# Seventeen of the up projection's 22 gate/value pairs by seven half products instead of eight

## The chip, the core and the metric

The kernel runs on one core of a Trainium2 chip. The metric is device time in microseconds for one execution of the whole program, median of several runs; lower is better. TensorE (PE) multiplies, VectorE (DVE), ScalarE (ACT) and GpSimd (POOL) work on rows of 128 partitions, SyncE (SP) issues most DMAs. Every engine takes its instructions in program order and waits on semaphores where the program says so.

## The reference

Two layers of a decoder on 520 tokens (512 of a prompt, 8 samples), model width 1024. The part that the change touches is the ConvFFN of each layer:

```
xn    = rms_norm(x, ffn_pre)                       # 520 x 1024
gate, value = xn @ w_up[:, :2816], xn @ w_up[:, 2816:]
h     = gelu(conv3(gate) + bias) * value           # causal convolution over tokens, width 3
x     = x + rms_norm(h @ w_down, ffn_post)
```

The last two gate rows of the prompt and of every sample are outputs too. All matrices are float32.

## The kernel before, in words

Activations lie transposed: 128 features on the partitions, 520 tokens in the free dimension, kept as two halves of 260 (`HALF`). A weight matrix comes as chunks of 128 x 1024 floats (512 KB), one DMA each on SP, into a ring of three (`ring`). Each float32 operand is split in two of a reduced format: ScalarE copies a chunk to its high part (`split_w` in the scalar block, L1479), VectorE subtracts that from the chunk to get the low part (L1882, in place of the chunk), and `w_hi`, `w_lo` count them. A product is then three matmuls: high by high, high by low, low by high (L925, L926, L927 in `dense_tile`), each of 128 x 128 weights by 260 columns. An output tile (128 features, both halves) takes 8 blocks x 2 halves x 3 = 48 matmuls in a pair of PSUM banks; three such pairs take turns, and `evac_a`, `evac_v` tell TensorE when one is free.

The up projection has 22 pairs of tiles, gate i and value i. `dense_front` makes the first three tiles in an order that lets it start before all of the input is there (L946, L947, L955); `dense_tile` the other 41. The input's halves are `hm_hi` (ScalarE, L1492) and `hm_lo` (VectorE, L1896); the norm's factor `rstd` is applied after the product. For pair i VectorE takes the gate out of PSUM (L2420), runs the convolution (`conv`: L2404 to L2408, of which the two with 8 columns are for the samples), multiplies it after ScalarE's gelu (L1801) by `rstd` (L2431), and by the value tile out of PSUM (L2433) into `hf`. Two weight splits a pair lie between. GpSimd does only three small copies a pair, the rows that are outputs (L1832 to L1834), and `ffn_t` tells VectorE that the buffer `gx` may be overwritten two pairs later. `hf` is split in its turn: the first 11 blocks (`EARLY`) during the up projection, the others right after it (L1483 on ScalarE, L1889 on VectorE), since their high parts lie where `hm_hi` and `hm_lo` were. The down projection then has 8 tiles over 22 blocks, three chunks each, and its first tile waits for each block's low part (`s_lo`).

The order on each engine is written out in the loops. The chunks of up and down go through the ring in one sequence, each DMA waiting for the tile three before it (`w_used`).

## Time and profile before

| | us |
|---|---|
| median of 3 runs | 2001.44 |
| lowest, highest | 2000.12, 2002.71 |
| span of the profiled execution, first to last instruction | 1997.6 |
| up projection of the first layer, all but its first three tiles | 624.1 to about 860.7 |
| the same of the second | about 1613 to 1850 |

The profiled execution is told by its span; what lies around the span is in the runs' times and not in the profile: 3.8 us between the span and the median. A row of the profile names an engine, the line of the kernel, the operation, what it writes and reads with shapes, and how often; then its time.

### The profile page before, as it was taken

The page shows a single profiled execution, that of the slowest core. Times are in us where ns is not written, and L with a number is a line of the kernel's source. Part 1 is how long each engine was busy: PE and PEld are TensorE (multiplying, and loading weights), DVE is VectorE, ACT ScalarE, POOL GpSimd, SP SyncE. Part 2 cuts the span into 40 slices and gives each one's busy share as a digit, 9 for nine tenths or more (in the row PEclk, how much of TensorE's full clock was granted, in tenths as well). Part 3 has the DMA queues.
Part 4 walks back from the last instruction along what each step waited for, and adds up shares of the span by engine and source line. Part 5 has one row for each costly group of instructions (what it writes and reads, how often), then busy time and mean ns, then how long its engine had stood idle before and what let it go on. Part 6 is the DMA issues. An engine that isn't in the chain of part 4 may idle for free.

```text
span 1997.6 us, 53462 instructions
## 1 busy us (share of the span) xinstructions
PE 1936.6 (97%) x22496; PEld 1795.0 (90%) x22496; DVE 1241.9 (62%) x2066; ACT 732.4 (37%) x1394; POOL 30.4 (2%) x143
## 2 busy tenths in 40 slices
PE   8999999999999999999999999999999999999997
PEld 7999888776799999999999998887677999999997
DVE  3475868888638665542355767688776476656323
ACT  3223345563634222232232234545636342222321
POOL 0000000000000000000000000000000000000000
PEclk9999999999999999999999999999999999999999
DMA  5225444144222332233342255333442222222332
GB/s 218 88 83 164 149 126 141 55 125 136 87 89 65 95 96 87 94 95 95 101 142 85 75 190 160 113 107 93 128 121 72 78 85 96 86 95 96 96 96 89
DMA packets 153010, 214.29 MB, mean 107 GB/s; under 512 B 18497, under 2 KB 118338, under 8 KB 151362
## 3 DMA queue, kind: packets, MB, share of 16 engines
q1 hardware_dynamic: 134050, 200.38, 31.8%
q10 hardware_dynamic: 18720, 10.49, 1.7%
q8 instruction: 177, 2.90, 0.6%
q14 instruction: 63, 0.52, 0.1%
HBM read 202.58 MB, written 16.59 MB: 110 GB/s over the span
## 4 chain that ended last, share of the span: by engine, by line
PE 77%; DVE 14%; ACT 3%; issue 2%; DMA 2%; ACTq 1%; SPq 0%; DVEq 0%
PE ps L925 18%; PE ps L927 18%; PE ps L926 18%; PE ps L1315 5%; PE ps L1193 1%; DMA ring<-in_w 1%; PE ps L1286 1%; PE ps L1182 1%; PE ps L946 1%; PE ps L947 1%; PE ps L1300 1%; DVE arena L2192 1%; DVE arena L2154 1%; PE ps L1279 1%; PE ps L1195 1%
## 5 line engine op out<-in xcount | busy, mean ns | idle before, releaser
L927 PE MATMUL ps<-hm_hi,ring_lo 128*128 128x260 f32 x1568 | 444.1, 283 | 0.0
L1882 DVE TENSOR_TENSOR ring_lo<-ring,ring_hi 128x1024 fp32r<-128x1024 f32 x130 | 159.3, 1225 | 303.5 <-ACT ring_hi L1479 301.7
L927 PEld LDWEIGHTS ps<-hm_hi,ring_lo 128*128 128x128 f32 x1568 | 296.2, 189 | 0.0
L925 PE MATMUL ps<-hm_hi,ring_hi 128*128 128x260 f32 x1008 | 285.5, 283 | 0.0
L926 PE MATMUL ps<-hm_lo,ring_hi 128*128 128x260 f32 x1008 | 284.6, 282 | 0.0
L1479 ACT ACTIVATE ring_hi<-ring 128x1024 fp32r<-128x1024 f32 x130 | 137.7, 1060 | 319.5 <-DMA ring<-in_w 311.5
L927 PE MATMUL ps<-hf_hi,ring_lo 128*128 128x260 f32 x704 | 198.9, 283 | 0.0
L927 PE MATMUL ps<-in_hi,ring_lo 128*128 128x260 f32 x704 | 198.8, 282 | 0.0
L925 PEld LDWEIGHTS ps<-hm_hi,ring_hi 128*128 128x128 f32 x1008 | 189.6, 188 | 1.8 <-issue 1.8
L926 PEld LDWEIGHTS ps<-hm_lo,ring_hi 128*128 128x128 f32 x1008 | 189.7, 188 | 0.0
L1882 DVE TENSOR_TENSOR ring_lo<-ring,extra_hi 128x1024 fp32r<-128x1024 f32 x64 | 78.4, 1225 | 154.2 <-ACT extra_hi L1479 153.0
L925 PE MATMUL ps<-hm_hi,extra_hi 128*128 128x260 f32 x496 | 140.3, 283 | 0.0
L926 PE MATMUL ps<-hm_lo,extra_hi 128*128 128x260 f32 x496 | 139.9, 282 | 0.0
L927 PEld LDWEIGHTS ps<-hf_hi,ring_lo 128*128 128x128 f32 x704 | 132.6, 188 | 0.0
L927 PEld LDWEIGHTS ps<-in_hi,ring_lo 128*128 128x128 f32 x704 | 132.6, 188 | 0.0
L925 PE MATMUL ps<-in_hi,ring_hi 128*128 128x260 f32 x448 | 128.8, 287 | 1.6 <-DVE ring_lo L1882 1.6
L1479 ACT ACTIVATE extra_hi<-ring 128x1024 fp32r<-128x1024 f32 x64 | 67.8, 1060 | 169.3 <-DMA ring<-in_w 166.6
L925 PE MATMUL ps<-hf_hi,ring_hi 128*128 128x260 f32 x448 | 127.2, 284 | 0.0
L926 PE MATMUL ps<-in_lo,ring_hi 128*128 128x260 f32 x448 | 126.6, 283 | 0.0
L926 PE MATMUL ps<-hf_lo,ring_hi 128*128 128x260 f32 x448 | 126.5, 282 | 0.0
L1716 ACT ACTIVATE arena<-ps,arena 128x128 f32<-128x128 f32 (+3 forms) x128 | 66.2, 526 | 97.6 <-DVEq L442 95.5
L1801 ACT ACTIVATE arena<-arena 128x520 f32<-128x520 f32 x44 | 28.2, 640 | 185.2 <-DVEq L442 185.2
(451 smaller groups left out, 4567.3 us busy)
## 6 DMA issues: line engine op xcount, KB each, us to landing
ring<-in_w SPq DMA_DIRECT2D x200, 512.0 KB, 3.5
extra<-in_kv_cmp SPq DMA_DIRECT2D x96, 128.0 KB, 2.3
arena<-in_kv_cmp SPq DMA_DIRECT2D x80, 128.0 KB, 2.4
slot<-in_kv_cmp SPq DMA_DIRECT2D x80, 128.0 KB, 2.4
out_win_old<-in_win SPq DMA_DIRECT2D x16, 511.0 KB, 4.2
slot<-in_k_sel SPq DMA_DIRECT2D x72, 64.0 KB, 2.0
extra<-in_k_sel SPq DMA_DIRECT2D x72, 64.0 KB, 1.9
arena<-in_v_sel SPq DMA_DIRECT2D x72, 64.0 KB, 2.0
```

What stands on the lines that cost most here:

```text
L925: mmul(out, wh, hi[:, k, cols], start=(k == 0), stop=False)
L926: mmul(out, wh, lo[:, k, cols], start=False, stop=False)
L927: last = mmul(out, wl, hi[:, k, cols], start=False, stop=(ci == len(chunks) - 1 and k == k1 - 1))
L946: mmul(ps[:, banks[i] + h, 0:HALF], w_high(l, n + i)[:, w], hi[:, k, cols], start=(k == 0), stop=False)
L947: last = mmul(ps[:, banks[i] + h, 0:HALF], w_low(l, n + i)[:, w], hi[:, k, cols], start=False, stop=False)
L1182: last = mmul(ps[r, 2, cj * CH:(cj + 1) * CH], gb[r, c, j, 0, :], ww[r, c, j, :], start=True, stop=True)
L1193: last = mmul(ps[r, 0, cj * CH:(cj + 1) * CH], qq[r, c, j, :], zz[r, c, j, :], start=True, stop=True)
L1315: last = mmul(out, w1ss[l][c][:, k, :], slot[:, :, c, k, :], start=(k == 0), stop=(k == STRIDE // 2 - 1))
L1479: A(w_high(l, n), w_place(l, n), ACT.Copy).then_inc(S["w_hi"], 1)
L1716: o.go(A(pp[:, g, cols], ps[:, 4 + g, cols], ACT.Exp, bias=nm[:, q:q + 1], accum_out=sums[:, q:q + 1]))
L1801: o.go(A(cv[:, i % 2, :], cv[:, i % 2, :], ACT.Gelu_apprx_tanh))
L1882: v.tensor_tensor(w_low(l, n), w_place(l, n), w_high(l, n), SUB).then_inc(S["w_lo"], 1)
```

## The change

Each pair of up is 256 output features (gate and value) by 1024 inputs by 520 tokens. It is taken as a 2 x 2 block product: outputs gate and value, inputs the first and second four blocks of 128 (`HK`), tokens the first and second half of 260. Strassen's scheme in Winograd's form gives the four output quarters (gate and value, each half of the tokens) by 7 products of quarter size instead of 8. A quarter product is 4 blocks x 3 = 12 matmuls of 260 columns. Pairs 0 to 4 (`PAIRS = 5`) stay as they were.

- GpSimd makes four sums of weight quarters a pair (`s1` to `s4`, 128 x 512 each), and once a layer the four sums of input quarters (`tf`, 128 x 1040 each), for which it first scales `x` (eight 128 x 520). It also takes over the multiplication by `rstd` (`weigh`).
- ScalarE makes the high part of each of the 7 quarters (`high`), copies PSUM banks into others on which a product then goes on accumulating (`seed` "b", "c"), or into SBUF ("p7", "u4"), and takes the convolution's first tap (`tap`).
- VectorE makes the 7 low parts (`low`), takes the gate out of PSUM by halves (`gate_half`), and adds value quarters from PSUM and SBUF (`val_first`, `val_second`).
- Only 4 blocks of `hf` are split during up (`EARLY = 4`), 18 after it. The chunks of the 17 pairs have slots of their own and their own semaphores. Several semaphores of the first part of the layer are merged (`side_pe`, `side_act`, `side_dve`), with the same waits.

```diff
+PAIRS = 5
+NG = FT - PAIRS
+HK = KB // 2
+LEAD = 4
+def seven_order():
+    out = [(0, "a11")]
+    for g in range(NG):
+        out += [(g, "s2"), (g, "a12"), (g, "s3"), (g, "s1")] + ([(g + 1, "a11")] if g + 1 < NG else []) + [(g, "a22"), (g, "s4")]
+    return out
+SEVEN = seven_order()
...
+        xg = nsa[:].rearrange("p n t -> p (n t)")[:, 0:KB * TOK].rearrange("p (k t) -> p k t", k=KB)
+        tf = hm[:].rearrange("p k t -> p (k t)").rearrange("p (i k t) -> p i k t", i=4, k=HK)
...
+        SEVEN_X = {"a11": ("b11", "a"), "s2": ("t2", "b"), "a12": ("b21", "a"), "s3": ("t3", "e"), "s1": ("t1", "c"), "a22": ("t4", "b"), "s4": ("b22", "c")}
...
+    def gate_load(g):
+        if g >= 2:
+            sp.wait_ge(S["q_pe"], SEVENS * l + SEVEN_AT[g - 2, "a12"])
...
+        sp.dma_start(gate_slot(l, g)[0], I["w"][l, C_UP + 2 * (PAIRS + g)]).then_inc(gate_in[g % 2], 16)
...
+    def product(q):
+        g, name = SEVEN[q]
+        by, letter = SEVEN_X[name]
+        pe.wait_ge(S["q_lo"], QUARTERS * l + TWINS + q + 1)
+        if name == "a11":
+            if g < 2:
+                pe.wait_ge(S["evac_v"], dense_n[0] - 2 + g)
+            else:
+                pe.wait_ge(S["q_gate"], 2 * (NG * l + g - 2) + 1)
+        elif name == "s2":
+            pe.wait_ge(S["q_seed"], SEEDS * l + 4 * g + 1)
+        elif name == "s3" and g >= 2:
+            pe.wait_ge(S["q_val"], 2 * (NG * l + g - 2) + 1)
+        elif name == "s1":
+            pe.wait_ge(S["q_seed"], SEEDS * l + 4 * g + 2)
+        elif name == "s4":
+            pe.wait_ge(S["q_seed"], SEEDS * l + 4 * g + 4)
+        out = ps[:, seven_bank(g, letter), 0:HALF]
+        (hi, lo), wl, wh = moving(by), quarter_full(l, g, name)[1], quarter_high(g, name)
+        for k in range(HK):
+            w = slice(k * P, (k + 1) * P)
+            new = name in ("a11", "s3") and k == 0
+            mmul(out, wh[:, w], hi[:, k, :], start=new, stop=False, skip_group_check=True)
+            mmul(out, wh[:, w], lo[:, k, :], start=False, stop=False, skip_group_check=True)
+            last = mmul(out, wl[:, w], hi[:, k, :], start=False, stop=(k == HK - 1), skip_group_check=True)
+        last.then_inc(S["q_pe"], 1)
+    for q in range(SEVENS):
+        product(q)
+    pe.wait_ge(S["q_gate"], 2 * NG * (l + 1) - 1)
+    pe.wait_ge(S["q_val"], 2 * NG * (l + 1))
...
+    def high(q):
+        if q >= SEVENS:
+            split_w(C_DOWN + q - SEVENS)
+            return
+        g, name = SEVEN[q]
+        if g >= 2:
+            act.wait_ge(S["q_pe"], SEVENS * l + SEVEN_AT[g - 2, name])
+        if name in SUM_AT:
+            act.wait_ge(S["q_sum"], SUMS * l + 1 + 4 * g + SUM_AT[name])
+        elif name == "a22":
+            val_landed(act, l, g)
+        else:
+            gate_landed(act, l, g)
+        A(quarter_high(g, name), quarter_full(l, g, name)[0], ACT.Copy).then_inc(S["q_hi"], 1)
+    def seed(kind, g):
+        bank = lambda letter: ps[:, seven_bank(g, letter), 0:HALF]
...
+        A(dst, src, ACT.Copy).then_inc(S["q_seed"], 1)
+    def tap(g):
+        i = PAIRS + g
+        act.wait_ge(S["q_gate"], 2 * (NG * l + g + 1))
+        act.wait_ge(S["ffn_h"], FT * l + i - 1)
+        A(cv[:, i % 2, 0:SEQ], gx[:, i % 2, 0:SEQ], ACT.Identity, scale=C("cw0", i), bias=C("cb", i)).then_inc(S["q_tap"], 1)
+    def gelu(g):
+        i = PAIRS + g
+        act.wait_ge(S["ffn_c"], FT * l + i + 1)
+        A(cv[:, i % 2, :], cv[:, i % 2, :], ACT.Gelu_apprx_tanh).then_inc(S["ffn_act"], 1)
...
+    seed("b", 0)
+    for g in range(NG):
+        at = LEAD + 7 * g
+        high(at)
+        seed("c", g)
+        high(at + 1)
+        if g:
+            tap(g - 1)
+        high(at + 2)
+        seed("p7", g)
+        high(at + 3)
+        seed("u4", g)
+        high(at + 4)
+        if g:
+            gelu(g - 1)
+        if g + 1 < NG:
+            seed("b", g + 1)
+        high(at + 5)
+        if g + 1 < NG:
+            high(at + 6)
+    tap(NG - 1)
+    gelu(NG - 1)
+    act.wait_ge(S["q_pe"], SEVENS * (l + 1))
+    act.wait_ge(S["q_val"], 2 * NG * (l + 1))
     for k in range(EARLY, FT):
-        act.wait_ge(S["ffn_h"], FT * l + k + 1)
+        act.wait_ge(S["ffn_h"], FT * l + k + 1 if k < 12 else FT * (l + 1) - (k < FT - 1))
         split_s(hf_hi, hf, k)
...
+    pool.wait_ge(S["norm_h"], KB)
+    pool.wait_ge(S["kv_stored"], 16 * (l + 1))
+    for k in range(KB):
+        o.go(g.tensor_scalar(xg[:, k, :], x[:, k, :], C("ffn_pre", k), None, ALU.mult))
+    o.settle()
+    first, second = xg[:, 0:HK, :], xg[:, HK:KB, :]
+    o.do(g.tensor_tensor(tf[:, 0, :, :], first[:, :, HALF:TOK], first[:, :, 0:HALF], ALU.subtract))
+    o.do(g.tensor_tensor(tf[:, 1, :, :], second[:, :, HALF:TOK], tf[:, 0, :, :], ALU.subtract))
+    o.go(g.tensor_tensor(tf[:, 2, :, :], second[:, :, HALF:TOK], first[:, :, HALF:TOK], ALU.subtract))
+    o.go(g.tensor_tensor(tf[:, 3, :, :], second[:, :, 0:HALF], tf[:, 1, :, :], ALU.subtract))
+    o.tell(S["q_sum"])
+    rs = rstd[:].rearrange("p h n -> p (h n)")
...
+    def total(n, name):
+        full = lambda of: quarter_full(l, n, of)[0]
+        if name == "s1":
+            gate_landed(pool, l, n)
+            val_landed(pool, l, n)
+        if name != "s3":
+            if n >= 2:
+                pool.wait_ge(S["q_pe"], SEVENS * l + SEVEN_AT[n - 2, name])
+            elif n:
+                pool.wait_ge(S["w_used"], C_UP + 2 * PAIRS)
+        if name == "s1":
+            g.tensor_tensor(full("s1"), full("a21"), full("a22"), ALU.add).then_inc(S["q_sum"], 1)
+            return
+        pool.wait_ge(S["q_sum"], SUMS * l + 4 * n + SUM_AT[name])
+        if name == "s2":
+            g.tensor_tensor(full("s2"), full("s1"), full("a11"), ALU.subtract).then_inc(S["q_sum"], 1)
+        elif name == "s3":
+            g.tensor_tensor(full("s3"), full("a11"), full("a21"), ALU.subtract).then_inc(S["q_sum"], 1)
+        else:
+            g.tensor_tensor(full("s4"), full("a12"), full("s2"), ALU.subtract).then_inc(S["q_sum"], 1)
+    def weigh(n):
+        i = PAIRS + n
+        pool.wait_ge(S["ffn_act"], FT * l + i + 1)
+        g.tensor_tensor(cv[:, i % 2, :], cv[:, i % 2, :], rs, ALU.mult).then_inc(S["q_cvr"], 1)
+    last_rows(0)
+    last_rows(1)
+    for name in ("s1", "s2", "s3", "s4"):
+        total(0, name)
+    for i in range(2, PAIRS):
+        last_rows(i)
+    total(1, "s1")
+    total(1, "s2")
+    for n in range(NG):
+        if n + 1 < NG:
+            total(n + 1, "s3")
+            total(n + 1, "s4")
+        if n:
+            last_rows(PAIRS + n - 1)
+            weigh(n - 1)
+        if n + 2 < NG:
+            total(n + 2, "s1")
+            total(n + 2, "s2")
+    last_rows(FT - 1)
+    weigh(NG - 1)
...
+    def low(q):
+        if q >= SEVENS:
+            split_w(C_DOWN + q - SEVENS)
+            return
+        g, name = SEVEN[q]
+        dve.wait_ge(S["q_hi"], QUARTERS * l + TWINS + q + 1)
+        dve.wait_ge(S["q_sum"], SUMS * l + 1 + 4 * g + SUM_USED[name])
+        full, lo = quarter_full(l, g, name)
+        v.tensor_tensor(lo, full, quarter_high(g, name), SUB).then_inc(S["q_lo"], 1)
+    def gate_half(g, h):
+        i = PAIRS + g
+        letter, product = ("a", "a12") if h == 0 else ("c", "s4")
+        dve.wait_ge(S["ffn_t"], FT * l + i - 1)
+        dve.wait_ge(S["ffn_c"], FT * l + i - 1)
+        dve.wait_ge(S["q_pe"], SEVENS * l + SEVEN_AT[g, product])
+        v.tensor_tensor(gx[:, i % 2, 2 + h * HALF:2 + (h + 1) * HALF], ps[:, seven_bank(g, letter), 0:HALF], rstd[:, h, :], MUL).then_inc(S["q_gate"], 1)
+    def val_second(g):
+        dve.wait_ge(S["q_seed"], SEEDS * l + 4 * g + 4)
+        dve.wait_ge(S["ffn_h"], FT * l + PAIRS + g - 1)
+        v.tensor_tensor(val_sum[g % 2][:, 1, :], ps[:, seven_bank(g, "e"), 0:HALF], u4_copy[g % 2], ADD).then_inc(S["q_val"], 1)
+    def val_first(g):
+        dve.wait_ge(S["q_seed"], SEEDS * l + 4 * g + 3)
+        dve.wait_ge(S["q_pe"], SEVENS * l + SEVEN_AT[g, "a22"])
+        v.tensor_tensor(val_sum[g % 2][:, 0, :], ps[:, seven_bank(g, "b"), 0:HALF], p7_copy[g % 2], ADD).then_inc(S["q_val"], 1)
...
+    for q in range(LEAD):
+        low(q)
+    for g in range(NG):
+        at = LEAD + 7 * g
+        low(at)
+        if g:
+            gate_half(g - 1, 1)
+            conv_sample(g - 1, 0)
+        low(at + 1)
+        if g:
+            conv_sample(g - 1, 1)
+        low(at + 2)
+        gate_half(g, 0)
+        if g:
+            conv_second(g - 1)
+        low(at + 3)
+        if g:
+            conv_third(g - 1)
+        low(at + 4)
+        low(at + 5)
+        val_second(g)
+        if g + 1 < NG:
+            low(at + 6)
+        val_first(g)
+        if g:
+            ffn_out(g - 1)
+    gate_half(NG - 1, 1)
+    conv_sample(NG - 1, 0)
+    conv_sample(NG - 1, 1)
+    conv_second(NG - 1)
+    conv_third(NG - 1)
+    split_s(hf_lo, hf, hf_hi, FT - 1, EARLY)
+    ffn_out(NG - 1)
+    split_s(hf_lo, hf, hf_hi, FT, FT - 1)
```

## Rows read from the trace of the kernel before

**Rows 1.** The page: busy time by engine, granted clock, chain that ended last.
```profile
PE 1936.6 (97%) x22496; PEld 1795.0 (90%) x22496; DVE 1241.9 (62%) x2066; ACT 732.4 (37%) x1394; POOL 30.4 (2%) x143
PE 77%; DVE 14%; ACT 3%; issue 2%; DMA 2%; ACTq 1%; SPq 0%; DVEq 0%
```
**Rows 2.** Waits of TensorE, 624 to 880 us: total, times, longest.
```profile
PE ps L925 <- ACTq L1794: 0.2, 1, 0.2
```
**Rows 3.** Stretches: from:to, length, each engine's busy us (instructions), granted clock, DMA share, GB/s.
```profile
612.71:640.00 27.29, 27.11 (x273) 26.57 (x272) 23.30 (x38) 10.72 (x15) 2.72 (x9) 1.00 0.29 97
680.00:720.00 40.00, 40.00 (x336) 40.00 (x336) 26.11 (x40) 11.46 (x14) 2.56 (x12) 1.00 0.30 93
```
**Rows 4.** GpSimd in order of time (start, duration): 1st copy of two pairs running.
```profile
809.91 0.19 POOL L1832 COPY arena<-arena 128x2 f32<-128x2 f32 x1 [10.86 <-DVEq L442]
821.43 0.19 POOL L1832 COPY arena<-arena 128x2 f32<-128x2 f32 x1 [10.88 <-DVEq L442]
```
**Rows 5.** Groups on VectorE, 616 to 862 us: count, busy us, mean ns, idle before.
```profile
L1882 DVE TENSOR_TENSOR ring_lo<-ring,ring_hi 128x1024 fp32r<-128x1024 f32 x28 | 34.3, 1226 | 50.7 <-ACT ring_hi L1479 50.3 <-DVE arena L2433 0.2
L2408 DVE SCALAR_TENSOR_TENSOR arena<-arena,par 128x520 f32<-128x520 f32 x22 | 16.7, 760 | 0.8
L2406 DVE SCALAR_TENSOR_TENSOR arena<-arena,par 128x512 f32<-128x512 f32 x22 | 16.5, 752 | 0.8
L2433 DVE TENSOR_TENSOR arena<-arena,ps 128x520 f32<-128x520 f32 x21 | 14.6, 696 | 0.7
L1889 DVE TENSOR_TENSOR hf_lo<-arena,hf_hi 128x520 fp32r<-128x520 f32 x11 | 7.7, 700 | 1.6
L1857 DVE COPY rstd<-ps 128x260 f32<-128x260 f32 x1 | 0.4, 430 | 0.1
```
**Rows 6.** Groups on ScalarE, 616 to 862 us, the same columns.
```profile
L1479 ACT ACTIVATE ring_hi<-ring 128x1024 fp32r<-128x1024 f32 x28 | 29.7, 1061 | 50.1 <-DMA ring<-in_w 46.0 <-ACT arena L1801 3.0 <-PE ps L955 1.1
L1801 ACT ACTIVATE arena<-arena 128x520 f32<-128x520 f32 x22 | 14.1, 640 | 93.1 <-DVEq L442 93.1
L1483 ACT ACTIVATE hf_hi<-arena 128x520 fp32r<-128x520 f32 x14 | 8.6, 626 | 3.0 <-DVEq L2435 2.5 <-PE ps L927 0.4
L1470 ACT ACTIVATE rstd<-ps 128x260 f32<-128x260 f32 x1 | 0.4, 387 | 1.7 <-PE ps L998 1.7
```
**Rows 7.** Groups on GpSimd, the whole span.
```profile
L1832 POOL COPY arena<-arena 128x2 f32<-128x2 f32 x44 | 8.2, 186 | 1814.8 <-DVEq L442 1814.8
L1817 POOL MEMSET ones<- 128x128 f32 x1 | 0.2, 205 | 0.3 <-POOLq L2541 0.3
L1819 POOL MEMSET tiny<- 128x2 f32 x1 | 0.1, 101 | 0.0
```
**Rows 8.** VectorE and GpSimd in order of time, at 630, 706 and 729 us.
```profile
630.35 1.24 DVE L1882 TENSOR_TENSOR ring_lo<-ring,extra_hi 128x1024 fp32r<-128x1024 f32 x1
630.45 1.19 POOL L1833 COPY arena<-arena 128x8 f32<-128x8 f32 x1
...
706.42 0.56 DVE L2404 TENSOR_SCALAR arena<-arena,par 128x512 f32<-128x512 f32 x1 [0.15 <-DVE arena L2420]
706.64 0.39 POOL L1834 COPY arena<-arena 128x8 f32<-128x8 f32 x1
...
729.67 0.19 POOL L1834 COPY arena<-arena 128x8 f32<-128x8 f32 x1
729.81 0.55 DVE L2404 TENSOR_SCALAR arena<-arena,par 128x512 f32<-128x512 f32 x1 [0.50 <-DVE arena L2420]
```
**Rows 9.** VectorE in order of time before the dense tiles of up start.
```profile
612.09 0.70 DVE L2388 TENSOR_TENSOR x<-x,arena 128x520 f32<-128x520 f32 x1
612.71 3.44 DVE L1896 SCALAR_TENSOR_TENSOR hm_lo<-x,par,hm_hi 128x520 fp32r<-128x520 f32 x5
```
**Rows 10.** VectorE and ScalarE in order of time, end of up.
```profile
860.87 5.92 ACT L1483 ACTIVATE hf_hi<-arena 128x520 fp32r<-128x520 f32 x11 [0.44 <-PE ps L927]
863.28 6.80 DVE L1889 TENSOR_TENSOR hf_lo<-arena,hf_hi 128x520 fp32r<-128x520 f32 x11 [0.25 <-ACT hf_hi L1483]
```
**Rows 11.** The page's DMA issues: count, KB each, median us to landing.
```profile
ring<-in_w SPq DMA_DIRECT2D x200, 512.0 KB, 3.5
```

More of the change, by code:

```diff
@@ L70, with roped_at @@
 KEEP = 5
+PAIRS = 5
[8 more added lines that the diff above has]
+SEVEN = seven_order()
+SEVEN_AT = {key: i + 1 for i, key in enumerate(SEVEN)}
+SIDE_PE = {"gate": 1, "rope": 1, "vt": 9, "cmpp": 9}
+SIDE_ACT = {"gate_sg": 1, "gate_ev": 2, "staged": 3, "vt": 4, "cmpp_p": 5, "cmpp_t": 6, "kcp": 7}
+SIDE_DVE = {"staged": 2, "ready": 9, "cmpp_x": 10, "cmpp_h": 11}
+def roped_at(r):
+    return r if r == 1 else r + 1
+SUM_AT = {"s1": 1, "s2": 2, "s3": 3, "s4": 4}
+SUM_USED = {"a11": 3, "a12": 4, "a22": 1, "s1": 2, "s2": 4, "s3": 3, "s4": 4}
+SEVENS = len(SEVEN)
+SEEDS = 4 * NG
+SUMS = 4 * NG + 1
+TWINS = 4
+QUARTERS = SEVENS + TWINS
 COLS = {}
@@ new lines, in val_place, with val_slot, quarter_full @@
+        def val_place(g):
+            return (0, 2, 1)[g % 3]
+        def val_slot(l, g):
+            i = val_place(g)
+            if i == 0:
+                return t_raw[:, 1024:2048], t_r[:, 1024:2048]
+            if i == 1:
+                return ring[:, ring_of(l, 1), :], ring_lo[:, ring_of(l, 1), :]
+            return e_f[:, 0:1024], e_r[:, 0:1024]
+        def quarter_full(l, g, name):
+            half = lambda pair, i: tuple(a[:, 512 * i:512 * (i + 1)] for a in pair)
+            if name in ("a11", "a12"):
+                return half(gate_slot(l, g), name == "a12")
+            if name in ("a21", "s3", "a22"):
+                return half(val_slot(l, g), name == "a22")
+            if name == "s4":
+                return half((extra, x_r), 0 if g % 2 else 6)
+            return half((ring[:, ring_of(l, 2), :], ring_lo[:, ring_of(l, 2), :]) if g % 2 else (n_f, n_r), name == "s2")
@@ L1554, in _ @@
                         o.go(A(gate_rows[0:24, :], gate_rows[0:24, :], ACT.Tanh, scale=0.5))
[L1555 removed]
+                        o.tell(S["side_act"])
                     if m > NT:
@@ L1794, in _ @@
                     act.sem_inc(S["evac_a"], 1)
+                    if m in (4, 5, 6, 7):
+                        twin_high((1, 2, 0, 3)[m - 4])
+                    if m >= 8:
+                        for q in range(LEAD // 2):
+                            high(LEAD // 2 * (m - 8) + q)
                     if m % 2:
@@ L1827, in _, with last_rows @@
                 S = SL[l]
-                for i in range(FT):
-                    pool.wait_ge(S["evac_v"], N_IN + KB + 2 * i + 1)
+                C = columns(l)
+                pool.wait_ge(S["norm_h"], KB)
[10 more added lines that the diff above has]
+                rs = rstd[:].rearrange("p h n -> p (h n)")
+                def last_rows(i):
+                    if i < PAIRS:
+                        pool.wait_ge(S["evac_v"], N_IN + KB + 2 * i + 1)
+                    else:
+                        pool.wait_ge(S["q_gate"], 2 * (NG * l + i - PAIRS + 1))
                     if i == 0:
```

259 lines of the change are left out of this document (197 added, 62 removed).

## The prediction

> **What bounds the kernel now.** I read the page's busy times and granted clock first, then TensorE's waits, stretches, and groups by engine. TensorE is busy 97% of the span, and it holds 77% of the chain that ended last [rows 1]. From 624 us to 880 us, nearly all of the first layer's up projection and the start of down, it waits 0.2 us in all [rows 2], at full granted clock [rows 3]. One gate/value pair, 96 matmuls, takes 821.43 - 809.91 = 11.52 us [rows 4], so 0.120 us a matmul. In a 40 us stretch of it VectorE is busy 26.1, ScalarE 11.5, GpSimd 2.6 [rows 3]. So the stage goes at TensorE's pace, and fewer matmuls would shorten it by their full time as long as the others keep up. VectorE has the least room.
>
> **What is removed.** A pair falls from 96 matmuls to 7 x 12 = 84, 10.08 us at the same pace. There are 17 pairs in each of two layers: 34 x 1.44 = 49 us at most.
>
> **What each engine must do in 10.08 us.**
> ScalarE: 7 copies of 512 columns at about 0.54 us (11 of 520 took 5.92 us back to back [rows 10]), 4 seeds of 260 at 0.39, tap and gelu at 0.64 [rows 6]: 6.6 us. It has room. SP issues the same two 512 KB loads a pair, each landing 3.5 us after issue [rows 11], and each slot is free some eight products before its next use, so they are hidden.
> VectorE: 7 low parts of 512 at 0.62 (11 of 520 in 6.80 us [rows 10]) = 4.3; the last two taps 0.75 + 0.76, `ffn_out` 0.70, four quarters out of PSUM at 0.43 [rows 5], two of 8 columns at about 0.25: 8.7 us. It would just fit, if nothing holds it up.
> GpSimd: four sums of 512 and `weigh` of 520, none of which the trace shows. A memset of 128 columns takes 205 ns and one of 2 takes 101, so 0.83 ns a column for one pass; a small copy takes 0.19 us [rows 7]. With two passes (two inputs read in turn, the write beside them) 512 columns take 0.19 + 0.85 = 1.04 us, with three passes 1.46. I take 1.25, between them. From below, VectorE's own pace for it would be 0.69. Five are 6.2 us, with the small copies 7.0. Taken alone, it is hidden too.
>
> **Why they don't add up side by side.** The small copies on GpSimd show something else. In the ordinary case they take 0.19 us. At 630.45 one of 8 columns takes 1.19 us, and it ends 0.05 us after a VectorE subtraction of two SBUF tensors that began 0.1 us earlier [rows 8]; the second layer has the same. Under the first tap, 706.42 to 706.98, the third copy takes 0.39 and ends 0.05 us after it [rows 8]; 41 of the 44 pairs have this. Once, at 729, the copies come first, and the tap starts 0.14 us into the last copy, after 0.50 us of idle time instead of 0.15 [rows 8]. So instructions of the two engines exclude one another, in both directions, for most of their length. The Trainium skill, "SBUF — State Buffer", section "SBUF: two separate sides", says it as a rule: VectorE with two SBUF inputs and GpSimd reading SBUF share a port pair under an exclusive lock held for the whole instruction, and the loser waits; by that rule the two engines' times add, the trace agrees (1.19 us for a 0.19 us copy), and its sum is the one that follows.
>
> In the change almost everything heavy on VectorE has two SBUF inputs: 7 low parts, two taps, `ffn_out`, together 7 x 512 + 512 + 520 + 520 = 5136 columns a pair. The slope between 1024 and 520 columns is (1226 - 700)/504 = 1.04 ns [rows 5]. If an instruction holds the other off only while it streams, VectorE holds 5.3 us and GpSimd 5 x 1.06 + 0.1 = 5.4: 10.7 us a pair. If it holds for all but 0.05 us of its recorded time, VectorE holds 7 x 0.64 + 0.70 + 0.71 + 0.65 = 6.5 and GpSimd 5 x 1.2 + 0.5 = 6.5: 13.0 us. The 1.19 us copy lies between (it got in some 0.1 us before the other's end). I take the middle, 11.8 us. Each low part is then late for its product, and the product waits: `low` of the next quarter is queued behind it on VectorE, and the taps, `gate_half` and `val_first` behind that. A pair so costs 11.8 against 11.52 before: +0.3 x 34 = +10 us, with bounds of 34 x (10.7 - 11.5) = -27 and 34 x (13.0 - 11.5) = +51.
>
> "GPSIMD Engine Reference" of the Trainium skill, section 3.1, gives 4497 ns for a two-input addition of 2048 columns; an estimate by it is 1.12 us for 512, which would take 0.65 us off a pair and 22 us off the total. No row here shows it.
>
> **The edges of the stage, each layer.**
> Front. GpSimd starts when `x` is complete, at 612.8 [rows 9]. Eight scalings of 520 (one pass 0.62, two 1.05; I take 0.8) and four sums of 1040 (1.92 to 2.78; 2.35) are 15.8 us. In 612.7 to 640 VectorE is already busy 23.3 of 27.3 us [rows 3], of which some 17 in instructions with two SBUF inputs, beginning with the low parts of the input [rows 9]. 17 + 15.8 is 5.5 us more than there is; I take 6 us (bounds 0, if nothing excludes, and 12). Who waits: the first tiles for `hm_lo`, and gate tile 2's evacuation for `last_rows(0)`, which is queued behind the sums.
> First product. Its low part is queued on VectorE behind pair 4's evacuation, two low parts of 1040 (2.4 us), convolution 2.6, gelu 0.64, two multiplications 1.4 and itself 0.7: 8.5 us from the end of the gate tile, against 5.8 us of value tile. 3 us late, 4 with GpSimd between, and 0.6 for the first seed.
> End. VectorE's `low` runs on into the three down chunks before `val_second` and `val_first` of the last pair. These chunks load only after the last but one pair's `s4`: 3 loads take about 7.5 us (3.5 + 2 x 2), high 1.06, low 1.23, two quarters 0.9 = 11 us, against six products, 8.6 us. Down starts 3 us late, 4 with exclusion. Then block 4 of `hf` waits for half a gate, tap, two taps, gelu, high and low, 4.5 us and more, against 4 ready blocks of 6 matmuls, 2.9 us: 2.5 us. The other 17 blocks follow at 0.62 us, faster than TensorE's 0.72 a block.
> Sum: 6 + 4.6 + 4 + 2.5 = 17 us. The first three pairs run at TensorE's 10.08, since GpSimd made their sums ahead: -4.5. So +12.5 a layer, +25 us.
>
> **Sum.** +10 + 25 = +35 us on the profiled execution (span 1997.6, so about 2033), which stands 3.8 us under the median of the runs; on that median 2001.4 + 35 = 2036 us. The merged semaphores keep their waits: 0.
>
> **Rivals.**
> A. The exclusion does not bite: VectorE gets in between, or isn't held up by a long GpSimd instruction. The 17 pairs go at TensorE's pace. -49, edges 3.0 + 0.6 + 2.9 + 2.2 = 8.7 a layer: -49 + 17 = -32, 1970 us. For it: 8.7, 6.6 and 7.0 us all fit in 10.08, and GpSimd's hold on VectorE is seen once in 44 pairs, by copies of 0.19 us. Against it: both directions show it.
> B. Exclusion with the short holds: 10.7 to 10.9 a pair, -24, edges 10 a layer: about 1998 us, from 1980 to 2005. For it: the copy's early entry; GpSimd's unseen cost could be its lower bound.
> C. GpSimd is itself the bound, whatever VectorE does: from 1.8 us a sum on (5 x 1.8 + 0.8 = 9.8, with its own waits over 10.08). At 2.2 us it is 12 us a pair and, with exclusion, over 15: 2085 us and more. Against it: three passes are 1.46 us. This and the forecast are on the slower side, by the same chain (GpSimd and VectorE before TensorE).
> That the change doesn't do what it says is not one: the seven products per pair are written out.
>
> **Chances.** Forecast 0.55, its own range 2005 to 2075; A 0.28; B 0.11; C 0.06. B splits evenly about "within 0.2%" (4 us, about what a measurement of this kernel can tell from no change) and faster. So faster 0.34, same 0.06, slower 0.60. Range 1966 to 2075: it takes in A's centre and the forecast's bounds and leaves out C and A's better half.
>
> **What would show it.** Right: GpSimd's sums recorded at over 1.3 us where VectorE works beside them and VectorE's 512-column subtractions spread from 0.69 upward or starting late; TensorE's waits in 670 to 860 us all on low parts, 1 to 2 us a pair; a period of 11.5 to 12.5 us between the same instruction of two pairs; down's first tile broken up. Wrong: a period of 10.1 us with TensorE's share at 99%, or sums that take 0.7 us. The granted clock should stay full; if it falls in the stage, a wait is longer than I think.

## The result and the profile after

| | before | after |
|---|---|---|
| median of 4 runs, us | 2001.82 | 2077.10 |
| lowest, highest | 2000.12, 2002.71 | 2072.77, 2077.39 |
| span of the profiled execution | 1997.6 | 2071.0 |

The ratio is 1.0364 (95% interval 1.035 to 1.0379): 75.3 us slower, where the forecast was 35 us slower and the range ended at 2075. Of the spans the difference is 73.4 us.

The page's busy times and its chain of waits by engine, answering to [rows 1]:

```profile
PE 1922.9 (93%) x22088; PEld 1762.9 (85%) x22088; DVE 1428.0 (69%) x2278; ACT 861.5 (42%) x1742; POOL 368.4 (18%) x337
...
PE 54%; DVE 30%; issue 7%; ACT 4%; DMA 2%; ACTq 1%; DVEq 1%; SPq 0%; POOL 0%
```

TensorE's share of the chain falls from 77% to 54%, VectorE's doubles, and GpSimd, which works twelve times as long as before, is not in the chain at all: it does its harm through VectorE.

Where [rows 2] had 0.2 us, the waits of TensorE in the first layer, 600 to 960 us, are now these (instruction, what released it, total, times, longest):

```profile
PE ps L1635 <- DVE ring_lo L2789: 11.7, 7, 1.7
PE ps L1635 <- DVE n_r L2789: 11.2, 7, 1.7
PE ps L1635 <- DVE t_r L2789: 7.2, 1, 7.2
PE ps L1099 <- issue: 5.9, 2, 4.3
PE ps L1099 <- DVE ring_lo L2249: 5.6, 3, 2.2
PE ps L1099 <- DVE hf_lo L2256: 1.3, 1, 1.3
...
PE ps L1635 <- ACT ps L2041: 0.6, 1, 0.6
```

L1635 is the first matmul of a quarter product, L2789 a quarter's low part. The first two rows are one pattern, since the slots take turns: once a pair, 14 times, the product `s1` waits 1.67 us for its low part (the first time 1.2). The third row is the first product. "issue" holds the start of down (4.25 us) and one gate tile. The same waits, within 0.1 us, stand in the second layer, but for the 1.3 in down.

Stretches (columns as in [rows 3]): the front, the beginning of the pairs, their regular part, and two after long waits in the second layer:

```profile
612.71:640.00 27.29, 25.43 (x257) 24.70 (x256) 25.22 (x26) 8.09 (x12) 26.81 (x13) 1.00 0.39 145
...
680.00:720.00 40.00, 36.81 (x294) 35.82 (x293) 31.61 (x44) 19.79 (x41) 22.12 (x20) 0.98 0.27 94
...
700.00:825.00 125.00, 107.79 (x847) 102.89 (x846) 115.73 (x161) 63.34 (x130) 89.33 (x80) 1.00 0.24 85
...
1705.20:1713.00 7.80, 7.20 (x32) 6.93 (x33) 2.80 (x5) 2.16 (x5) 0.00 (x0) 0.51 0.00 0
...
1918.50:1924.00 5.50, 5.49 (x24) 5.25 (x24) 3.78 (x7) 3.00 (x6) 1.75 (x4) 0.50 0.00 0
```

In the regular part VectorE is busy 115.73 of 125 us, GpSimd 89.33. A pair takes 12.52 us (waits at 732.84 and 757.83 lie two pairs apart). VectorE's share of that is 11.6 us, and it stands idle for 0.93.

One pair on VectorE, and GpSimd beside it, in order of time:

```profile
774.36 0.74 DVE L2834 SCALAR_TENSOR_TENSOR arena<-arena,par 128x520 f32<-128x520 f32 x1
775.03 0.68 DVE L2789 TENSOR_TENSOR n_r<-nsa,e_r 128x512 fp32r<-128x512 f32 x1
776.63 1.09 DVE L2789 TENSOR_TENSOR t_r<-arena,x_r 128x512 fp32r<-128x512 f32 x1 [0.93 <-ACT x_r L2014]
777.64 0.42 DVE L2804 TENSOR_TENSOR b<-ps,b 128x260 f32<-128x260 f32 x1
777.98 1.46 DVE L2789 TENSOR_TENSOR ring_lo<-ring,e_r 128x512 fp32r<-128x512 f32 x1
779.37 0.41 DVE L2810 TENSOR_TENSOR b<-ps,b 128x260 f32<-128x260 f32 x1
779.71 1.45 DVE L2841 TENSOR_TENSOR arena<-arena,b 128x520 f32<-128x520 f32 x1
781.08 1.75 DVE L2789 TENSOR_TENSOR n_r<-nsa,e_r 128x512 fp32r<-128x512 f32 x1
...
783.09 0.94 DVE L2818 TENSOR_SCALAR arena<-arena,par 128x8 f32<-128x8 f32 x1
...
775.86 1.32 POOL L2181 TENSOR_TENSOR arena<-arena,rstd 128x520 f32<-128x520 f32 x1 [2.98 <-ACT arena L2054]
777.13 1.76 POOL L2167 TENSOR_TENSOR ring<-arena 128x512 f32<-128x512 f32 x1
779.04 1.56 POOL L2171 TENSOR_TENSOR ring<-ring 128x512 f32<-128x512 f32 x1
780.68 1.60 POOL L2173 TENSOR_TENSOR arena<-ring,arena 128x512 f32<-128x512 f32 x1
```

The same subtraction of 512 columns takes 0.68 us at 775.03, with GpSimd idle, and 1.09, 1.46 and 1.75 with a GpSimd sum beside it. The evacuations with one input in PSUM (L2804, L2810) keep their 0.42. So the waiting time is recorded inside the instruction: VectorE looks busy while it is held up. Five instructions a pair meet GpSimd: the four rows of 1.09, 1.46, 1.45 and 1.75 us and the tap of 8 columns at 783.09 (0.94 us; 0.28 in the run without sums below). Each loses 0.4 to 1.1 us, 3.7 us together.

The chain of waits through that idle time:

```profile
774.36 0.76 DVE arena L2834
...
775.14 0.02 ACT arena L2054
...
775.68 0.37 ACT ps L2041
776.06 0.55 ACT x_r L2014
...
777.98 1.46 DVE ring_lo L2789
```

It contains no matmul: VectorE's third tap releases ScalarE's gelu (0.64 us), behind which ScalarE makes a seed and the high part that VectorE's next low part needs. In the regular part the period is a loop of VectorE with this one detour, and TensorE has dropped out.

The front, GpSimd and the VectorE instructions that it holds up:

```profile
612.48 14.73 POOL L2132 TENSOR_SCALAR nsa<-x,par 128x520 f32<-128x520 f32 x8 [610.89 <-DVE x L2755]
627.29 3.24 POOL L2135 TENSOR_TENSOR hm<-nsa 128x1040 f32<-128x1040 f32 x1
...
636.72 2.60 POOL L2138 TENSOR_TENSOR hm<-nsa,hm 128x1040 f32<-128x1040 f32 x1
...
628.16 2.93 DVE L2870 TENSOR_TENSOR arena<-arena,rstd 128x520 f32<-128x520 f32 x1
...
634.37 2.67 DVE L2771 TENSOR_SCALAR arena<-arena,par 128x512 f32<-128x512 f32 x1
636.96 2.38 DVE L2772 TENSOR_SCALAR arena<-arena,par 128x8 f32<-128x8 f32 x1
```

The preparation takes 27 us, not 15.8, and an operation of 8 columns takes 2.38 us.

### The profile page after: what moved, and what is told of

It reads as the page before. It is cut to its first block, busy times and chain, and to the rows that moved or that the text cites. A ratio compares the mean times of both kernels' runs of the same rounds, so it can differ in the third digit from the quotient of the medians.

```text
span 2071.0 us, 54036 instructions
## 1 busy us (share of the span) xinstructions
PE 1922.9 (93%) x22088; PEld 1762.9 (85%) x22088; DVE 1428.0 (69%) x2278; ACT 861.5 (42%) x1742; POOL 368.4 (18%) x337
## 4 chain that ended last, share of the span: by engine, by line
PE 54%; DVE 30%; issue 7%; ACT 4%; DMA 2%; ACTq 1%; DVEq 1%; SPq 0%; POOL 0%
PE ps L1099 9%; PE ps L1101 9%; PE ps L1100 9%; PE ps L1489 5%; DVE arena L2841 2%; DVE ring_lo L2789 2%; PE ps L1367 1%; DMA ring<-in_w 1%; PE ps L1460 1%; DVE hf_lo L2256 1%; PE ps L1635 1%; PE ps L1356 1%; DVE arena L2834 1%; PE ps L1120 1%; PE ps L1474 1%
## 5 line engine op out<-in xcount | busy, mean ns | idle before, releaser
L2249 DVE TENSOR_TENSOR ring_lo<-ring,ring_hi 128x1024 fp32r<-128x1024 f32 x84 | 104.1, 1240 | 200.8 <-ACT ring_hi L1688 198.7
L1688 ACT ACTIVATE ring_hi<-ring 128x1024 fp32r<-128x1024 f32 x84 | 88.8, 1059 | 211.4 <-DMA ring<-in_w 208.2
L1101 PE MATMUL ps<-hm_hi,ring_lo 128*128 128x260 f32 x480 | 136.4, 284 | 0.0
L1635 PE MATMUL ps<-t_hi,e_r 128*128 128x260 f32 x288 | 84.9, 295 | 23.7 <-DVE n_r L2789 22.5
L1099 PEld LDWEIGHTS ps<-hf_hi,ring_hi 128*128 128x128 f32 x448 | 85.4, 191 | 8.5 <-issue 7.8
L1101 PEld LDWEIGHTS ps<-hm_hi,ring_lo 128*128 128x128 f32 x480 | 91.2, 190 | 0.0
L1099 PEld LDWEIGHTS ps<-in_hi,ring_hi 128*128 128x128 f32 x448 | 84.3, 188 | 2.6 <-issue 2.3
L1099 PE MATMUL ps<-hm_hi,ring_hi 128*128 128x260 f32 x272 | 78.2, 287 | 8.7 <-DVE ring_lo L2249 5.4
L1100 PEld LDWEIGHTS ps<-hf_lo,ring_hi 128*128 128x128 f32 x448 | 85.5, 191 | 0.0
L1100 PEld LDWEIGHTS ps<-in_lo,ring_hi 128*128 128x128 f32 x448 | 84.3, 188 | 0.3
```

Of the source, the lines that this page charges most:

```text
L1099: mmul(out, wh, hi[:, k, cols], start=(k == 0), stop=False)
L1100: mmul(out, wh, lo[:, k, cols], start=False, stop=False)
L1101: last = mmul(out, wl, hi[:, k, cols], start=False, stop=(ci == len(chunks) - 1 and k == k1 - 1))
L1635: mmul(out, wh[:, w], hi[:, k, :], start=new, stop=False, skip_group_check=True)
L1688: A(w_high(l, n), w_place(l, n), ACT.Copy).then_inc(S["w_hi"], 1)
L2249: v.tensor_tensor(w_low(l, n), w_place(l, n), w_high(l, n), SUB).then_inc(S["w_lo"], 1)
```

## The experiments

**Do the two engines exclude each other, and with what inputs?** The kernel before, with a block of single instructions ahead of its work (the edit in short).

```diff
+for _ in range(4): o.do(g.tensor_tensor(tc, ta, tb, ALU.subtract))      # GpSimd alone, 512 columns
+for _ in range(2): o.do(g.tensor_scalar(tc, ta, 2.0, None, ALU.mult))
+for _ in range(6): o.do(g.tensor_tensor(tc, ta, tb, ALU.subtract))      # beside each kind of VectorE
...
+o.do(v.tensor_tensor(dc, da, db, SUB))               # x4 alone, then x7 beside GpSimd
+o.do(v.tensor_tensor(dc, ps[:, 5, :], db, SUB))      # x7
+o.do(v.tensor_scalar(dc, da, 2.0, 1.0, MUL, ADD))    # x7
+o.do(v.memset(dc, 1.0))                              # x7
```

> The kernel before with a block of single instructions ahead of the first weight split, on 512 columns: GpSimd alone (4 two-input subtractions, 2 one-input scalings), VectorE alone (4 two-input subtractions), then GpSimd's subtraction six times beside seven of VectorE, of four kinds: two SBUF inputs, one PSUM and one SBUF input, one SBUF input, memset. Only the trace counts. Theory X (the two engines exclude one another): GpSimd alone about 1.2 us, VectorE alone 0.69; beside two SBUF inputs the recorded times of one or both rise so that start to start the two alternate, 1.8 us a pair of them; beside a PSUM input or a memset both stay as alone. Theory S (GpSimd is slow by itself and nothing excludes): GpSimd alone 1.55 us as in the changed kernel, VectorE 0.69 everywhere.

GpSimd and VectorE in order of time:

```profile
5.10 5.32 POOL L1830 TENSOR_TENSOR nsa<-nsa 128x512 f32<-128x512 f32 x4 [3.50 <-DVE nsa L1859]
10.51 3.07 POOL L1832 TENSOR_SCALAR nsa<-nsa 128x512 f32<-128x512 f32 x2
18.05 10.02 POOL L1837 TENSOR_TENSOR nsa<-nsa 128x512 f32<-128x512 f32 x6 [4.48 <-DVE nsa L1864]
28.77 16.34 POOL L1837 TENSOR_TENSOR nsa<-nsa 128x512 f32<-128x512 f32 x12 [0.69 <-DVE nsa L1868]
...
13.68 2.87 DVE L1862 TENSOR_TENSOR nsa<-nsa 128x512 f32<-128x512 f32 x4 [8.66 <-POOL nsa L1832]
...
17.91 10.71 DVE L1868 TENSOR_TENSOR nsa<-nsa 128x512 f32<-128x512 f32 x7
28.66 5.04 DVE L1870 TENSOR_TENSOR nsa<-ps,nsa 128x512 f32<-128x512 f32 x7
36.86 8.99 DVE L1872 TENSOR_SCALAR nsa<-nsa 128x512 f32<-128x512 f32 x7 [3.16 <-POOL nsa L1837]
```

Alone, a VectorE subtraction takes 2.87 / 4 = 0.72 us and a GpSimd one 1.33. Side by side GpSimd's six take 1.67 us each and VectorE's seven 1.53 on average; one of the seven has no partner, and (10.71 - 0.72) / 6 gives 1.67 for the others too. With an input in PSUM VectorE keeps 0.72; with one SBUF input it goes from 0.55 [rows 8] to 1.28. Had they simply taken turns, a pair of instructions would last 0.72 + 1.33 = 2.05 us; it lasts 1.67 (1.8 was expected), so starts and ends overlap. By the Trainium skill, "SBUF — State Buffer", section "SBUF: two separate sides", the loser is blocked for the whole of the other's instruction; these rows show the exclusion, but a fifth less than that.

**Is exclusion enough to slow a kernel in which nothing else is changed?** The kernel before, its pairs with 96 matmuls each, and five idle subtractions a pair on GpSimd.

```diff
                     o.tell(S["ffn_t"])
+                    for _ in range(5 if 5 <= i < FT - 1 else 0):
+                        o.do(g.tensor_tensor(fl[:, 1040:1552], fl[:, 0:512], fl[:, 520:1032], ALU.subtract))
```

> The kernel before, whole and unchanged in its matmuls, plus five subtractions of 512 columns on GpSimd for each of pairs 5 to 20 of both layers, on a buffer that nobody reads; nobody waits for them. VectorE works 7.5 us a pair there (26.1 of 40 us by a period of 11.52). Exclusion: each of the five costs VectorE about 1.07 us, as the changed kernel's did, so 7.5 + 5.4 = 12.9 us against 11.52: up to +1.3 us a pair, times 32 = +43 us; less where GpSimd's instructions fall into VectorE's idle time, so 2015 to 2050 us. Rival (the seven-product order, its semaphores or ScalarE's part make the 12.5 us period, and exclusion only accompanies it): 2000 to 2004 us, VectorE's instructions as long as before.

2056.02 us, ratio 1.0266 (1.0216 to 1.0317): 53.5 us slower, by instructions that no one waits for. A pair takes 12.85 us (VectorE's evacuation starts at 768.07 and 780.92); the total lies 6 us above the expected range. A stretch of it, TensorE's wait, VectorE's wait in one pair, and two of its groups on VectorE, 700 to 820 us:

```profile
760.00:800.00 40.00, 38.64 (x321) 38.28 (x320) 33.26 (x32) 8.71 (x10) 27.83 (x25) 1.00 0.31 93
...
PE ps L925 <- DVE ring_lo L1887: 17.6, 14, 3.2
...
775.52 1.58 DVE L1887 TENSOR_TENSOR ring_lo<-ring,ring_hi 128x1024 fp32r<-128x1024 f32 x1 [2.02 <-ACT ring_hi L1479]
...
L2413 DVE SCALAR_TENSOR_TENSOR arena<-arena,par 128x520 f32<-128x520 f32 x9 | 16.8, 1862 | 0.3
...
L2412 DVE SCALAR_TENSOR_TENSOR arena<-arena,par 128x8 f32<-128x8 f32 x9 | 11.3, 1252 | 0.0
```

The third tap went from 760 ns [rows 5] to 1862, and the tap of 8 columns takes 1252. VectorE waits for no result of GpSimd in these pairs. The rival, that the order of the seven products or ScalarE's part in it makes the long period, falls. But that 7.5 + 5.4 = 12.9 came out is luck. In the pair from 768.07 to 780.92 VectorE is busy 10.33 us, 2.8 more than its own 7.5 and not 5.4 more, and it stands idle for 2.5, of which 2.02 are one wait for ScalarE: the late third tap delays ScalarE's gelu, and the high part that VectorE splits next is queued behind it.

**How much does each sum cost?** Each sum replaced by one memset of its buffer, for all four sums, and for `s3` and `s4` only.

```diff
-                    if name == "s1":
-                        g.tensor_tensor(full("s1"), full("a21"), full("a22"), ALU.add).then_inc(S["q_sum"], 1)
...
+                    g.memset(full(name), 0.5).then_inc(S["q_sum"], 1)
```

These kernels leave out all or two of the sums, so their products are not the real ones.

> The changed kernel, but each of the four weight sums is one memset of the same 512 columns (the sums are left out, the semaphores stay). Theory X: the exclusion goes with the reads, the period of a pair falls from 12.5 to 10.1 to 10.8 us, and about 34 x 1.9 = 55 to 65 us go: 2010 to 2020 us. Rival P (TensorE's restarts at the product boundaries set the period, not GpSimd): no more than 10 us go.

> The changed kernel with the sums s3 and s4 replaced by one memset each (weights are then not the real ones); s1, s2 and the multiplication by rstd stay real. Exclusion with a price for each real sum: from 12.52 us a pair (four sums) and a floor of 10.33 (none), two sums less give 12.52 - 2 x 1.07 = 10.4 us, about the floor; waits of 0 to 0.4 us a pair, 2000 to 2015 us. Rival (the pair is held by the place of one certain sum, s1 or s2, ahead of the product that waited, and not by VectorE's total): 12.0 us or more a pair, 2055 us or more.

All four: 1999.51 us, ratio 0.9983 (0.997 to 0.9996). Two: 2036.27, ratio 1.0168 (1.0114 to 1.0221). The stretch of regular pairs in the one without sums, and one of the two rows of TensorE's waits for `s1`'s low part in the one with two:

```profile
690.00:840.00 150.00, 150.00 (x1254) 150.00 (x1253) 127.63 (x238) 96.08 (x195) 55.75 (x118) 1.00 0.30 99
```
```profile
PE ps L1635 <- DVE ring_lo L2792: 4.1, 7, 0.6
```

Without sums TensorE never pauses and a pair takes 10.06 us (GpSimd's first copies start at 722.71 and 732.76); VectorE is busy 8.6 of them. Two sums make it 11.35, four 12.52: 0.6 us a sum. So all four matter, not one at a certain place. The price of 1.07 expected for each was too high. VectorE's busy time goes from 8.6 to 10.0 and 11.6 us a pair, 0.7 to 0.8 a sum; of that a part is taken out of its idle time, which is 1.5, 1.3 and 0.9 us. The 10.33 us that the expectation of the second took as the floor was an average over all 17 pairs and held the slow start told below.

A first version of this, with three memsets to a sum so that GpSimd was occupied about as long as by a real one:

> As e1_one_memset, but three memsets for each sum, one after the other, so that GpSimd is busy about as long as with the sums (3 x 0.55 us) and reads nothing. Theory X: only reading instructions exclude VectorE, so the time is that of e1_one_memset to within 10 us, 2010 to 2025. Theory S (GpSimd's own length is the bound): back near 2077 us.

2028.11 us, ratio 1.0123 (1.0093 to 1.0154), between the two expectations. It separates less than meant: GpSimd itself, busy 35.5 of 40 us, became late with the sums. It does show VectorE at 31 of 40 us, 8.6 a pair as with one memset a sum, beside a GpSimd that works more than in the changed kernel and whose memsets read nothing.

**The same work all on VectorE, and the multiplication by `rstd` there.** The first moves the four sums and the multiplication, the second the multiplication alone. This part of the edit is in both:

```diff
...
-                    dve.wait_ge(S["q_cvr"], NG * l + g + 1)
+                    dve.wait_ge(S["ffn_act"], FT * l + i + 1)
+                    o.do(v.tensor_tensor(cv[:, i % 2, :], cv[:, i % 2, :], rs, MUL))
```

> The whole computation, with the four weight sums and the multiplication by rstd on VectorE instead of GpSimd; the input sums stay on GpSimd. VectorE then has 8.7 + 5 x 0.62 = 11.8 us a pair plus waits for its own results, some 12.2, with nothing to exclude it. Theory X (the two engines' times add anyway): no slower than the changed kernel, period 11.9 to 12.4, 2055 to 2075 us. Theory S: VectorE becomes the bound by more than GpSimd was, period 13 and over, 2085 us or more.

> The whole computation; only the multiplication by rstd goes back from GpSimd to VectorE. From the probe, an instruction of GpSimd beside one of VectorE costs 1.67 us for the two, VectorE's alone 0.72. A pair then has 4 x 1.67 + 7 x 0.65 instead of 5 x 1.67 + 5 x 0.65 us under exclusion: 0.4 us less, 34 x 0.4 = 14 us, 2060 to 2068 us. Rival S (VectorE's own work is the bound, GpSimd's share hidden): 0.7 us more a pair, 2100 us.

2090.80 us, ratio 1.0438 (1.0414 to 1.0462), and 2096.51, ratio 1.0458 (1.043 to 1.0486). Both miss the range of the theory, and both come out at the figures of the rival S: 2085 or more with a period of 13, and about 2100. S as a mechanism, that nothing excludes, is refuted by the probe, so the misses need another reason, and the traces have it. With everything on VectorE nothing is blocked there, yet a pair takes 13.07 us: VectorE is busy 11.4 (22.75 in the two pairs from 793.8 to 819.9 us) and idle 1.7, of which 1.4 are two waits for ScalarE, 0.93 behind the gelu and 0.47 at another high part. The expected 12.2 had left these out. So the 0.93 is there with and without exclusion. A subtraction of 512 columns costs VectorE 0.6 to 0.7 us there, about what a sum on GpSimd costs it. Moving only the multiplication back to VectorE cost 0.6 us a pair more. In the changed kernel it starts in VectorE's idle time (775.86 above) and holds up only one low part, by 0.4 us. Moved, it adds its 0.7 to VectorE's own work, and the blocking does not fall: in three pairs running, from 757 us, VectorE's instructions are 4.0, 3.3 and 3.8 us longer than alone, against 3.7 before. Now the big taps are among them (1.83 and 1.81 us).

**The idle 0.93 us.** One thing moved on ScalarE, everything else as in the changed kernel.

```diff
-                    if g:
-                        gelu(g - 1)
                     if g + 1 < NG:
                         seed("b", g + 1)
                     high(at + 5)
+                    if g:
+                        gelu(g - 1)
```

> The changed kernel, whole computation, one thing moved on ScalarE: gelu of the pair before goes behind the next seed and the next high part instead of ahead of them. In the changed kernel the chain of waits in the 17 pairs is VectorE without a break but for one detour: third tap, then ScalarE's gelu 0.54, seed 0.37, high part 0.55, then the low part on VectorE, which stood idle 0.93 us for it. If the chain is right, VectorE's idle time of 0.93 a pair goes (up to 0.93 x 14 paced pairs x 2 layers = 26 us), less what a later gelu makes GpSimd's multiplication and the four sums behind it later: period 11.6 to 12.1 us, 2050 to 2068 us. Rival (the period is held by GpSimd's sums and their chain through the slots, VectorE's idle time is only slack): 12.5 us as before or more, since the multiplication on GpSimd starts 0.9 us later: 2077 to 2100 us.

2068.98 us, ratio 1.0328 (1.0308 to 1.0348). A stretch of it:

```profile
760.00:800.00 40.00, 36.07 (x275) 33.80 (x276) 39.77 (x54) 20.78 (x43) 27.77 (x26) 1.00 0.23 80
```

The idle time is gone: VectorE is busy 39.77 of 40 us. But the period only fell to 12.36 (11.6 to 12.1 expected), and the gain was 8 us of a possible 26, just short of the expected range. The shorter period makes 28 x 0.16 = 4.5 of the 8; the start of down came 1.2 us a layer sooner as well. Instead of the idle time another VectorE instruction (the tap of 8 columns, now 1.25 us instead of 0.22) is caught by GpSimd's last sum. The order of GpSimd's sums against VectorE's work sets how much is blocked: VectorE's busy time is 3.0 us a pair above that of the run without sums in the changed kernel, and 3.7 in this one. It is not a constant of the instructions.

**The edges.** First the preparation of the input sums cut to 8 columns and less, then its scalings moved to ScalarE, then the low parts of down's first three chunks put behind the last values.

```diff
-                    o.go(g.tensor_scalar(xg[:, k, :], x[:, k, :], C("ffn_pre", k), None, ALU.mult))
+                    o.go(g.tensor_scalar(xg[:, k, 0:8], x[:, k, 0:8], C("ffn_pre", k), None, ALU.mult))
...
```
```diff
...
+                for k in range(KB // 2, KB):
+                    o.go(A(xg[:, k, :], x[:, k, :], ACT.Copy, scale=C("ffn_pre", k)))
...
```
```diff
...
-                    low(at + 4)
-                    low(at + 5)
+                    if g < NG - 1:
+                        low(at + 4)
+                        low(at + 5)
...
                 gate_half(NG - 1, 1)
+                low(SEVENS)
...
```

> The changed kernel with GpSimd's preparation of the input sums cut to 8 columns an instruction (the products then take wrong input sums); all else stays. In the changed kernel GpSimd is at it for 27 us, and TensorE then loses 1.7, 2.2, 1.6 and 7.2 us up to the first product. Theory F1 (the preparation holds VectorE back): 8 to 10 us a layer go, 2057 to 2062 us. Rival F2 (the low parts of the input sums and the chain of pair 4 on VectorE do it): at most 3 us a layer, 2070 us or more.

2064.14 us, ratio 1.0302 (1.027 to 1.0334). The three waits of the first tiles (1.7, 2.2, 1.6 us) are gone, 5.5 us a layer; the 7.2 us before the first product stay. That is between the two expectations, and puts the price of the preparation at 13 us for both layers.

> The whole computation; the eight scalings of x go from GpSimd (14.7 us of its 27) to ScalarE, four ahead of the norm's root and four behind its broadcast. Theory F1: GpSimd is done with the input sums some 12 us earlier, and 3 to 6 us a layer go: 2065 to 2071 us. Rival F2: no more than 2 us a layer, and the norm may come 1 us later.

2078.03 us, ratio 1.0368 (1.0342 to 1.0393). No gain: the waits of the first tiles became one of 7.3 us for VectorE, and the first product's fell to 4.3.

> The whole computation; only on VectorE the low parts of the three down chunks are moved behind the last values and the last gate half, where TensorE waited 4.3 us for them at the start of down. If the order on VectorE is what down waits for: 3 to 4 us a layer go, 2069 to 2071 us. If it is the loads of the chunks (they start only after the last but one pair's last product): less than 1 us a layer.

2078.39 us, ratio 1.037 (1.0342 to 1.0397). No gain: down starts after 3.7 us instead of 4.25, and what it waits for is now the chunk's low part itself. Less than 1 us a layer is what the expectation had for the loads, but they are not shown to be the cause: in the changed kernel the three chunks have landed by 882.97 us, 2.4 us before the last product of up ends.

**Nearly all that excludes taken out at once**: the multiplication by `rstd` and the three small copies a pair stay. This kernel too leaves out the sums.

> The changed kernel with all four weight sums a pair as one memset, the input sums cut to 8 columns and less, and the low parts of down's first three chunks behind the last values (weights and input sums are then not the real ones). It takes out every instruction that excludes VectorE but the multiplication by rstd. Theory: 1999.5 (sums alone as memsets) less what the short preparation gave in the changed kernel, 2078 - 2064 = 13, less 0 to 2 for the end: 1984 to 1990 us. Left over the 49 us ideal (2001.8 - 49 = 1953) are then the first product, the end and the 0.25 us of restarts a pair. Rival (the edges too were all exclusion): 1953 to 1965.

1985.55 us, ratio 0.9925 (0.9905 to 0.9944), inside the expected 1984 to 1990. Even so it is 32 us above the ideal of 1953. TensorE's waits in its first layer, 600 to 900 us:

```profile
PE ps L1099 <- DVE ring_lo L2242: 4.9, 2, 3.1
PE ps L1635 <- DVE t_r L2782: 3.2, 1, 3.2
PE ps L1099 <- DVE hf_lo L2249: 1.0, 1, 1.0
...
PE ps L1635 <- ACT ps L2041: 0.6, 1, 0.6
```

9.7 us of waits a layer are edges that come with the change and not from GpSimd; the half clock after two of them (stretches of 15 matmuls at 0.22 us) adds 3 us. For the two layers that is some 25 of the 32 us. What the rest is was not settled.

## Why the prediction was wrong

The mechanism was the forecast one, and the side was right; the forecast size, 35 us, was less than half of the 75 that came. By the steps of the prediction, the first layer in us (measured between the same points of the two traces, waits as in the view above):

| step | forecast | measured |
|---|---|---|
| front: waits of the first tiles | +6 | +5.5 |
| first product | +4.6 | +8.4 |
| 17 pairs, first three included | +0.3 (4.8 - 4.5) | +11.4 |
| start of down | +4 | +4.3 |
| inside down | +2.5 | +5.2 |
| sum | +17.4 | +34.8 |

One sum of the forecast is off by itself: three pairs at 10.08 instead of the 11.8 already counted are -5.2 and not -4.5, which makes no difference to what follows.

**The pairs.** This is the step that failed. "I take the middle, 11.8 us" was the sum of what VectorE and GpSimd hold each other for; the period was 12.52, within the bounds of 10.7 to 13.0. Fourteen pairs at 0.72 more are 10 of the 11 us; the rest is the wait for the first seed, 0.55, and half clock after the first product's wait, ten matmuls at 0.22 us instead of 0.12. That the clock would fall if "a wait is longer than I think" stood among the signs, but with no price in the sum. VectorE's own work was nearly right (8.7 forecast, 8.6 in the run without sums, of which 0.4 is GpSimd's multiplication holding up a low part). The sums on GpSimd add 11.6 - 8.6 = 3.0 us to its busy time. That own and blocked time together give 11.6, nearly the forecast 11.8, is partly chance: the forecast added 5.9 us of VectorE's holds and 5.9 of GpSimd's and left out VectorE's evacuations from PSUM, while the trace has about 8 us of own work and 3.7 of blocking. What the sum lacked was the 0.93 us in which VectorE waits for ScalarE, of which the forecast only said that "it has room". VectorE, once it paces the pair, has no slack in which such a detour could hide. The gelu run shows that closing it brings back only 0.16 us of the period, as another instruction is blocked in its place: both terms belong to one loop, and neither is to be had alone. That exclusion starts this loop is shown by the kernel before with its idle subtractions: its order and its matmuls are the old ones, and it went from 11.52 to 12.85 us a pair, there too by blocking (2.8) and a wait for ScalarE that had been slack (2.0). Of the 2.44 us by which 12.52 stands over 10.08, 1.67 is the wait for `s1`'s low part. The other 0.77 is in gaps too short for the view of waits, up to 0.42 us from one matmul to the next at the start of a product.

**The GpSimd prices.** The scalings took 1.84 us each (14.73 / 8), over twice the 0.8 taken and above the upper bound of 1.05, the sums of 1040 columns 2.60 to 3.31 against 2.35. The probe shows why the bounds failed: a one-input instruction of 512 columns takes 1.53 us on GpSimd, more than the two-input one. "One pass" was the wrong model. The weight sums, 1.33 alone against 1.25, were close. That the front waits came out as forecast all the same (5.5 for 6) is luck: the preparation took 27 us for 15.8, but much of what it held up, such as the multiplication at 628.16 and the taps at 634.37 and 636.96, was on no product's path.

**The first product.** The queue on VectorE was as described, and the exclusion on top of it was put at 1 us. The runs split the wait of 7.24 us: 3.2 stay with next to nothing excluded (forecast 3), 2.8 belong to the first four weight sums, which GpSimd makes just then, and 1.2 more go with the preparation once the sums are gone. With the sums in place cutting the preparation left it at 7.2, so the two do not simply add. The 1.2 us up to 8.4 lie in the front's gaps too short for the view of waits.

**Down.** The start is right (4.3 for 4), though the loads took 6.1 us from the first issue to the last landing and not 7.5. Inside, block 4 waits 1.27 us (forecast 2.5), but the next tile's chunk, whose low part stands on VectorE behind 18 splits of `hf`, is 1.80 us late. Half clock after the start (15 matmuls, 1.45 us) makes up most of the rest. The forecast followed that queue only as far as the first tile.

**The rest of the program** has the same waits in the second layer and some 4 us more. Its up and down take 2 us more than those of the first layer: more matmuls go at half clock, 17 at 1709, which the first layer does not have, and 22 instead of 15 at 1919; the two rows at clock 0.51 and 0.50 above show them. The mixing part between the layers, where the change only merges semaphores, takes 3 us more than in the kernel before; in the first layer it cost nothing (up's dense tiles start at 624.28 against 624.68). There the granted clock is 0.50 for 13.7 us from 1234.9, and in the kernel before for 6.8 us from 1204.4. So 34.8 + 34.8 + 4 is the 73.4 of the spans. Why the clock stayed low longer there is open.

**The rivals.** A (exclusion does not bite, 1970) lost by the mechanism, and would have missed the time as well: with next to nothing excluded the chip gave 1985.6, 16 above A, since the edges are 16 us a layer and not 8.7. B's pace of 10.7 to 10.9 was not seen. C's time, 2085, was nearest but its cause is not: GpSimd is busy 89 of 125 us and waits 3 us a pair. The range ended below the forecast's own bounds: with the pairs alone at their upper bound, +51 for +10, the sum is 2077, and with the front's 12 us a layer 2089.

No experiment points to a version of this change that beats the kernel before. 1999.5 and 1985.6 are times without the sums.
